# Residual rows turned during the output projection, experts chosen for four groups at once, gate and up weights in 8 KB rows

## What is computed

```python
h = rms_norm(x); q, k, v, u = split(h @ w_in)
x = x + concat(attention(q, k, v, caches), pooling(u)) @ w_o
h = rms_norm(x, ln2_w)
lg = h @ w_rg + b_rg                    # 4 groups
g  = argmax(lg)
le = (h @ w_re + b_re)[group g]         # 4 experts in the group
top_v, top_i = top_k(le, 2)
gates = softmax(lg)[g] * softmax(top_v)
y = x + sum over the two experts e of gates[e] * (silu(h @ w_gate[e]) * (h @ w_up[e])) @ w_down[e]
```

## Time and profile before

| | us |
|---|---|
| median of 3 runs | 1116.34 |
| lowest and highest | 1115.23, 1116.45 |
| the profiled execution | 1114.88 |
| its span in the trace | 1113.0 |
| mean granted TensorE clock | 0.953 |

### The profile page before, as it was taken

How to read it: one execution, slowest core, us unless ns; L and a number is a source line. 1 busy time by engine, 2 the same in 40 slices (tenths; PEclk the granted TensorE clock), 3 DMA queues, 4 the chain that set the end, 5 groups by cost and what they waited for, 6 DMA issues and landing times.

```text
span 1113.0 us, 11421 instructions
## 1 busy us (share of the span) xinstructions
PE 983.6 (88%) x4851; PEld 581.4 (52%) x4851; DVE 268.5 (24%) x396; ACT 142.4 (13%) x325; POOL 19.5 (2%) x38
## 2 busy tenths in 40 slices
PE   5999999999989999999869788876898788978785
PEld 4777888878756667777543223322333233323232
DVE  2007999460423310101260001100010001100011
ACT  3011111211134420110200100000010000001000
POOL 0000000000010000000000000000000000000000
PEclk9999999999989999999969989989898889989898
DMA  9835999865469985284447999999999999999991
GB/s 348 292 127 194 329 404 363 322 252 157 162 243 357 353 312 179 85 302 151 159 195 284 399 389 410 395 408 390 398 400 384 412 387 408 391 399 407 387 372 40
DMA packets 126661, 343.47 MB, mean 309 GB/s; under 512 B 5181, under 2 KB 8439, under 8 KB 116391
## 3 DMA queue, kind: packets, MB, share of 16 engines
q1 hardware_dynamic: 108895, 296.19, 70.6%
q10 hardware_dynamic: 15408, 34.02, 8.3%
q0 software_dynamic: 2304, 12.48, 2.8%
HBM read 330.52 MB, written 11.98 MB: 308 GB/s over the span
## 4 chain that ended last, share of the span: by engine, by line
PE 69%; DMA 21%; SPq 4%; DVE 3%; issue 1%; ACT 1%; POOL 0%; ACTq 0%; DVEq 0%; POOLq 0%
PE PS L739 66%; DMA ring<-in_w_up 13%; SPq L430 4%; DMA ring<-in_w_gate 4%; DMA ring<-in_w_down 4%; PE PS L769 1%; DMA small<-in_small 1%; PE PS L805 1%; PE PS L996 1%; PE PS L754 0%; DVE HT L1479 0%; DVE Z L1479 0%; ACT zT L568 0%; DVE HT L1189 0%; ACT Z L602 0%
## 5 line engine op out<-in xcount | busy, mean ns | idle before, releaser
L739 PE MATMUL PS<-HT,ring 128*128 128x288 f32 x1536 | 382.1, 407 | 1.2 <-issue 0.6
L739 PEld LDWEIGHTS PS<-HT,ring 128*128 128x128 f32 x1536 | 288.3, 190 | 82.8 <-issue 4.9
L739 PE MATMUL PS<-ring,Z 128*64 128x512 f32 (+2 forms) x1072 | 252.7, 614 | 49.7 <-DMA ring<-in_w_up 22.9
L739 PEld LDWEIGHTS PS<-ring,Z 128*64 128x64 f32 (+2 forms) x1072 | 91.3, 146 | 201.3 <-issue 200.4
L739 PE MATMUL PS<-ring,HT 128*64 128x512 f32 x512 | 126.8, 655 | 24.0 <-DMA ring<-in_w_up 10.1
L739 PEld LDWEIGHTS PS<-ring,HT 128*64 128x64 f32 x512 | 44.8, 150 | 102.0 <-issue 102.0
L568 ACT ACTIVATE zT<-PS 128x288 f32<-128x288 f32 x48 | 19.7, 411 | 364.1 <-PE PS L739 364.1
L739 PE MATMUL PS<-Z,X 128*128 128x256 f32 x160 | 46.4, 423 | 9.3 <-DVE Z L1479 3.8
L1479 DVE TENSOR_TENSOR HT<-PS,small 128x512 f32<-128x512 f32 x24 | 16.6, 691 | 142.6 <-PE PS L739 142.6
L1538 DVE TENSOR_TENSOR Z<-Z,PS 128x512 f32<-128x512 f32 x8 | 5.5, 688 | 179.4 <-PE PS L739 179.4
L739 PEld LDWEIGHTS PS<-Z,X 128*128 128x128 f32 x160 | 29.8, 203 | 33.1 <-issue 16.2
(11 more groups left out here) (200 smaller groups left out, 517.9 us busy)
## 6 DMA issues: line engine op xcount, KB each, us to landing
ring<-in_w_gate SPq DMA_DIRECT2D x32, 2048.0 KB, 19.4
ring<-in_w_up SPq DMA_DIRECT2D x32, 2048.0 KB, 19.6
ring<-in_w_down SPq DMA_DIRECT2D x32, 2048.0 KB, 18.9
ring<-in_w_in ACTq DMA_DIRECT2D x12, 2048.0 KB, 17.4
ring<-in_w_o SPq DMA_DIRECT2D x8, 2048.0 KB, 11.7
ring<-in_cache_v SPq DMA_DIRECT2D x8, 1536.0 KB, 7.6
ring<-in_cache_v SPq DMA_DIRECT2D x32, 384.0 KB, 8.6
ring<-in_cache_k SPq DMA_DIRECT2D x24, 384.0 KB, 7.0
```

The lines of the kernel that those rows point to most:

```text
L739: return pe.matmul(out, lhsT, rhs, start=start, stop=stop, skip_group_check=True)
```

## The change

Five things are changed.

1. The residual rows are loaded into columns 2048 to 4095 of `z` (where v and u were) and turned by PE on their own (`turn_rows`), all within the column blocks (`XT_AT` says at which). DVE scales a turned block (`residual_turned`) and adds the projection's column block straight from `zTs` (`column_added`), so the router's product for block n follows three loop steps later and needs no turn of the sum. ACT's copy of block n waits for the sum of block n - 2. SP loads the rows before the second pair of w_o slots, no longer behind it. The square root's table is loaded ahead of the projection, the squares follow each chunk, the root follows the last square; the stores of the last part of x1 and of y's first value come behind the root and behind the logits' copy.
2. The router picks the maximum of the group logits and of each group's four experts in the same five operations, with 60 elements a partition where 12 stood. The second expert of each group is picked while PE makes the index table. The read indices are cast first, straight from PSUM; POOL gathers with them without a copy. The write indices have their own semaphore.
3. The first expert step begins after five of the eight selects; the other three and the gates' table follow its first and second `up`. PE's loop over two turns is written out.
4. Gate and up rows are loaded as four consecutive rows a partition, 8 KB in a row. So `select` takes every fourth column of the gathered rows, and a copy of ln2 in that order (`ln2R`) is loaded by 16 small DMAs at the head of POOL's program.
5. Three memsets of the router are done before the projection.

```diff
-    FIRST_BANKS = (7, 0, 1, 2)
+    FIRST_BANKS = (7, 2, 5, 1)
+    XT_AT = {2: (0, 1), **{n: (n - 1,) for n in range(3, 13)}, 13: (12, 13), 14: (14, 15)}
...
                 for e in range(2):
-                    sp.dma_start(ring[:, s + e, :].rearrange("p (c n) -> p c n", n=TILE),
-                                 w[e].rearrange("a (c p) n -> p (a c) n", p=P)[:, half * 8:half * 8 + 8, :]
+                    sp.dma_start(ring[:, s + e, :].rearrange("p (q n) -> p q n", n=RUN * TILE),
+                                 w[e].rearrange("a (q p c) n -> p (a q) (c n)", p=P, c=RUN)[:, half * 2:half * 2 + 2, :]
...
+        for r in range(4):
+            for q in range(DC // RUN):
+                pool.dma_start(ln2R[32 * r:32 * r + 32, RUN * q:RUN * q + RUN].unsqueeze(2),
...
         pool.wait_ge(x1_stored, 16 * 8)
+        pool.sem_inc(idx_copied, 2)
         for n in range(2):
-            stage_rows(n, 0, n, n + 1)
-            gather(n)
+            gather(n, n)
...
+                if n >= 2:
+                    act.wait_ge(x1T_done, n - 1)
                 block_out(n // 8, n % 8, wo_done, 4)
             if n % 4 == 2 and n > 4:
                 t = n // 4 - 1
-                act.wait_ge(wo_moved, 3 * t + 6)
                 for k, (t0, m) in enumerate(CHUNKS):
+                    act.wait_ge(wo_moved, 3 * t + 4 + k)
...
+                if n == 18:
+                    act.wait_ge(root_in, 8)
+                    act.activation(stat[:, 4:7], stat[:, 4:7], ACT.Sqrt).then_inc(roots, 1)
...
-        for n in range(DC + 6):
+        for n in range(DC + 3):
             if n < DC:
                 column_block(n // 8, n % 8, wo_done, wo_moved, BASE_WO, 4)
-            if 5 <= n < DC + 5:
-                x1_block(n - 5)
-            if n >= 6:
-                router_block(n - 6)
+            for c in XT_AT.get(n, ()):
+                turn_rows(c)
+            if n >= 3:
+                router_block(n - 3)
...
-                ins = mm(PS[:, bank, 256 * i:256 * i + 256], XG[n][:, c * P:(c + 1) * P], SR, True, True)
+                q0 = c // RUN * RUN * P
+                ins = mm(PS[:, bank, 256 * i:256 * i + 256], XG[n][:, q0 + c % RUN:q0 + RUN * P:RUN], SR, True, True)
...
+                if starts:
+                    for j in range(5):
+                        first_select(j)
+                    pe.wait_ge(htg_moved, 4)
...
                 up(k, 0, 4, 0, 1, g0_used)
+                if starts:
+                    for j in range(5, 8):
+                        first_select(j)
+                    pe.wait_ge(htg_moved, 8)
...
                 up(k, 0, 0, 1, 1, gate_done)
+                if starts:
+                    first_gates()
...
+        def column_added(c):
+
+            dve.wait_ge(zT_moved, 2 + 32 + c + 1)
+            dve.wait_ge(xT_moved, c + 1)
+            dve.scalar_tensor_tensor(x1T[:, c, :], zTs[:, c % 2, :], ln2T[:, c:c + 1], x1T[:, c, :],
+                                     ALU.mult, ALU.add).then_inc(x1T_done, 1)
...
+        step(dve.tensor_reduce(m5, L5, AX.X, ALU.max))
+        first_of(one5, L5, m5, best5, 5)
```

More of the change, by code:

```diff
@@ L54 @@
 CAP = 64
+RUN = 4
 NQ = 24
@@ L491, in stage_rows, with gather @@
             pool.wait_ge(idx_copied, nth)
-        def gather(n):
+        def gather(n, at=None):
+            at = 53 + 2 * n if at is None else at
             pool.indirect_dma_start(
                 out=XG[n], out_offset=None, in_=x1_scr,
-                in_offset=bass.IndirectOffsetOnAxis(ap=pidx[:, 53 + 2 * n:54 + 2 * n], axis=0),
+                in_offset=bass.IndirectOffsetOnAxis(ap=pidx[:, at:at + 1], axis=0),
             ).then_inc(gathered[n], 16)
@@ L1055, in turn_gates, with first_select, first_gates, experts @@
             ins.then_inc(sgt_done, 1)
-        def experts(it):
+        def first_select(j):
+            if j >= 4:
+                pe.wait_ge(htg_moved, j - 3)
+            select(0, j, FIRST_BANKS[j % 4])
+        def first_gates():
+            pe.wait_ge(gates_ready, 1)
+            pass_table(0, 4, 128, 232, 16)
+            pe.wait_ge(gates_ready, 2)
+            turn_gates()
+        def experts(it, first=False):
             def up(k, bank, s, w_half, nth, done):
@@ L1121, in experts @@
                 n, second = k // 2, k % 2
-                if not second:
+                starts = first and k == 0
+                if starts:
+                    for j in range(5):
+                        first_select(j)
+                    pe.wait_ge(htg_moved, 4)
+                elif not second:
                     pe.wait_ge(htg_moved, it * 16 + (8 * n + 8))
                 up(k, 0, 4, 0, 1, g0_used)
+                if starts:
+                    for j in range(5, 8):
+                        first_select(j)
+                    pe.wait_ge(htg_moved, 8)
                 if second:
@@ L1152, in _ @@
         pe.wait_ge(sr_ready, 1)
-        for j in range(8):
-            if j >= 4:
-                pe.wait_ge(htg_moved, j - 3)
-            select(0, j, FIRST_BANKS[j % 4])
-        pe.wait_ge(gates_ready, 1)
-        pass_table(0, 4, 128, 232, 16)
-        pe.wait_ge(gates_ready, 2)
-        pe.wait_ge(htg_moved, 5)
-        turn_gates()
-        with pe.Fori(0, 2) as it:
-            experts(it)
+        experts(0, first=True)
+        experts(1)
         pe.wait_ge(idx_ready, 1)
@@ L1348, in _ @@
         dve.tensor_scalar(stat[:, 4:7], stat[:, 0:3], 1.0 / D, EPS, ALU.mult, ALU.add).then_inc(root_in, 1)
-        step(dve.memset(R, 0.0))
         dve.wait_ge(roots, 6)
```

179 lines of the change are left out of this document (96 added, 83 removed).

## The result

| | before | after |
|---|---|---|
| median of 4 runs (us) | 1115.78 | 1091.22 |
| lowest and highest | 1113.64, 1116.45 | 1089.82, 1091.73 |
| profiled execution, its span | 1114.88, 1113.0 | 1091.73, 1089.9 |

After takes 0.9781 of the time of before [0.9764, 0.9798]: 24.6 us less, where 29.7 were forecast. On the chips of the experiments the kernel before ran between 1107 and 1118 us, with medians of 1111.6 (two chips) and 1115.5, and the intervals of the ratios reach 0.25 to 0.4% to either side (0.13 to 0.2% in the last set); where an experiment needs less than that, its trace is read, with times relative to a point within it.

A forecast was written before the change was run, and what follows sets the result against it. Bound: time to the first `up`'s end, then full DMA transfers, then PE's tail. Stream -26.2, front -4.0, head +0.5 give -29.7: 1085.2 us profiled, plus 1.5, 1086.6 median; own bounds 1080.5 to 1090 (0.62), with rivals up to 1097 over 0.9.

The forecast's parts named there:

- the front gives nothing: Rival: x1's store, y and weights hold the gather to 573 us, SP's first issue at 590.5; 1090.6 us, chance 0.20.
- sign of being wrong: Idle DMA mid-experts, select pairs over 1.13 us, 387 GB/s with 8 KB packets, or first gather landing after 573 us.
- signs of being right: Gate and up alone 420 GB/s or more at 1.01; 620-1040 us at 420; SP's load 585-588; projection's last block 549.
- the main term: Expert stream: gate and up rows in 8 KB move at 422 instead of 387 GB/s, 288.1 instead of 314.3 us, -26.2 us.
- PE as the bound: Rival in odd expert steps: weight loads at twice the time, pairs released late; 1092 to 1097 us, chance 0.12.
- 512 B is enough for line rate: Rival for the weight stream: 2 KB rows are as fast as 8 KB; about 1112.8 us, chance 0.03.
- so the stream stays fed: First expert step: second and third release at about 597 and 607 us, pairs in flight lasting to 598 and 608.
- the gather's issue, "no change": Router: +1.4 logits, +0.2 wider operations, -1.1 earlier indices, -0.6 POOL's copy; gather issued at 561.6 us, no change.
- -4.0: Everything before the expert stream: gather +1.9, five select pairs 7.6 us, first `up` -0.8; SP issues at 586.5 us.
- head and tail: Head: 16 small DMAs on POOL, +0.5 us, bounds 0 and +3. Tail: strided selects taken as nothing, at most 2 us.
- The projection's end: Six turns and three router products ahead of the last block: +5.0 us, projection ends at 548.8 us.
- The logits at +1.4: Behind the projection: DVE has the logits at about 555.6 instead of 554.22 us, bounds -1 and +3.

The follow-up runs named there:

- the last set: On one chip, before 1115.48 us: after 1091.74; gather ahead and gates' table later 1085.81; also with part 1 undone and small DMAs late 1082.67.
- selects first: After with part 3 undone, all eight selects and the gates' table ahead of the first expert product: 1095.64 us, ratio 0.9861 to before.
- the pair of experiments: After with part 4 undone (2 KB rows): 1111.43 us, ratio 0.9991; before with part 4 alone (8 KB rows): 1090.73 us, ratio 0.9806.
- weights behind the store: After, with SP issuing the first pair of up weights only when x1's last store has landed: 1090.3 us, ratio 0.9812 to before.
- the three kernels without that wait: After with first up weights behind x1's store (1090.3 us), with them behind the gathers (1087.6), and with part 1 undone (1086.55).
- weights behind the gather: After, with SP issuing the first pair of up weights only when both gathers have landed: 1087.6 us, ratio 0.9787 to before.

## Why the prediction was right, and where it missed

**The range held, its centre did not.** The forecast's own bounds ended at 1090 us. The 1091.2 us measured lie above them, beside the 1090.6 of the first rival, "the front gives nothing". Half of that rival happened: the gather landed at 575.4 us, past the 573 that were named as a sign of being wrong. The other half did not: SP's first load came 3.4 us earlier behind the block, and the time was missing in stream, head and tail. That the number is the rival's is chance. Another sign of being wrong also came, a select pair of 1.32 us where 1.13 was the limit, and the stream did not feel it. Of the signs of being right, the rates came (421 GB/s at 1.01; 422 in the middle), and SP's first load at 589.06 us missed its 585 to 588.

**Right: the bound and the size of the main term.** The stream was to become 26.2 us shorter, priced by the window of down rows. Where no release comes late it takes 447.8 us (selects first) and 447.9 (before with 8 KB rows) instead of 473.9: 25.9 to 26.1 us less. PE as the bound did not come about: at 86% busy the middle runs at 422 GB/s with a share of 1.01. The rule of the Trainium skill (DMA: Bandwidth & Descriptors, section Specifications) that 512 B is enough for line rate would have 2 KB rows as fast; the pair of experiments does not agree, with 387 against 424 GB/s.

**Wrong, 3.2 us: "so the stream stays fed".** The second release was put at about 597 us, with the first pair's bytes lasting to 598, and the third at 607. The comparison left out the time from issue to data, for which I had 1.5 us elsewhere: with it the two pairs' data come at 598.5 and 608.5, half a microsecond late by my own figures. By after's rows SP's second issue came at 600.03, 11.0 us behind the first at 589.06: three selects (3.17), the wait for DVE's scaling (0.78) and `up` (7.09). The third came at 611.45, 11.4 us behind that: the gates' table with its wait for DVE, and a product that ran at a granted clock of 0.76 (603 to 610 us) right behind that wait. I had taken distances of 10.5 and 10. A pair of 4.2 MB lasts 10 us at 422 GB/s, and each microsecond on top is a gap. The two gaps are 1.3 and 1.6 us by the windows. The second goes when the table moves behind the third product; the first stays then (201 GB/s from 594 to 596 us), and neither is there when the selects stay in front.

**Wrong in a part, 0.6 us in the sum: the gather's issue, "no change".** The index chain was counted, the store of x1 was not: the gather needs both. Before, it was issued at 548.39 and its landing was hidden behind the index chain; in after it took 9.94 us and ended 3 us behind the indices. The issue came 2.9 us later behind the block than before (528.7 and 525.8), where no change was forecast. POOL's copy, priced at -0.6, gave nothing either: where the store is out of the way POOL still starts 0.9 us behind the indices (560.57 to 561.51 with the weights behind the store), as it did with the copy (560.68 to 561.66). From the logits' turn to the gather's issue the router's change is worth 0.7 to 0.8 us (7.9 before; 7.1 to 7.2 in the three kernels without that wait), not 1.5. So the first select came 4.5 us later relative to the block (537.6 against 533.1), where +1.9 was forecast. The selects paid for it: 6.5 us from the first select to `up` instead of 12.7 (I had 7.6), and 7.1 instead of 8.8 from there to SP's issue. What they gained beyond my 7.6 and 8.0 us goes with the granted clock. Windows of before's first `up`, of after's five pairs and first `up`, and of the five pairs in the kernel with the weights behind the gather:

```profile
581.72:590.53 8.81, 8.81 (x35) 3.48 (x36) 0.25 (x2) 1.67 (x2) 0.18 (x1) 0.81 0.01 3
```

```profile
575.44:581.93 6.49, 6.49 (x20) 5.53 (x20) 2.77 (x4) 0.00 (x0) 0.00 (x0) 0.72 0.06 27
581.93:589.06 7.13, 7.13 (x34) 2.33 (x33) 0.69 (x1) 0.00 (x0) 0.00 (x0) 1.00 0.00 0
```

```profile
570.78:578.42 7.64, 7.64 (x21) 6.12 (x21) 2.77 (x4) 0.00 (x0) 0.00 (x0) 0.59 0.63 232
```

At a clock of 0.72 the five pairs took 6.5 us, at 0.59 the 7.6 that I had. The front's -3.4 agrees with -4.0 by luck: +2.6 us at the gather and -2.0 at the selects and `up` cancel. The row that showed the danger was read: the earlier trace rows, y's 8 KB packets at 2.12 MB beside 0.81 MB for the 2 KB weights. It was applied to the gather and not to the store that the gather waits for.

**Wrong, 1.4 us each: head and tail.** The head was put at +0.5 within 0 to 3: the small packets cost the loads beside them 37 GB/s over 10 us (380 and 343) and as much before that. I had written 2048 packets; by the pages' counts of those under 512 B (5181 before, 5694 after) there are 513 more. They carry 8 KB. The tail was put at 0 within 0 to 2: 1.1 us of its 1.4 is the stride; the other 0.3 us is not explained.

**The projection's end.** Forecast +5.0, measured +4.9 (544.67 - 35.91; 551.50 - 37.84 is 513.7 against 508.8). The logits at +1.4 came at +0.9 by PE's turn of them. Both terms held; what they were worth to the end was decided elsewhere.

The misses add up: 3.2 + 0.6 + 1.4 + 1.4 = 6.6 us, the difference between -29.7 and -23.1 of the spans. The step that failed most is the release order of the first step, 3.2 of the 6.6.

## What to carry to other kernels

Where windows of one trace show full DMA engines at two rates, the shape of the transfers is the price, and the window with the better shape forecasts what the other would cost, here to within about 1% of the gain. When a faster stream or a reordered start is costed, list for each transfer that a wait needs, also stores, what is issued ahead of it and how much of it there is, and compare each release plus the time from issue to data with the time at which the bytes in flight end. A step moved behind the first product of a loop should be put behind as many releases as its consumer allows.

## What the runs showed of the hardware

- Transfers of 2 KB rows run at 387 GB/s and of 8 KB rows at 421 to 424, both with full DMA engines; 49,152 fewer packets for the same 296.19 MB on SP's queue (108895 and 59743) go with a stream that is 26 us shorter.
- Weight loads with columns 16 bytes apart take 325 ns instead of 196; the earlier trace rows showed no sign of such a price on the moving side, though with no contiguous product of that size beside it.
- The granted clock is at its low level (0.50) when the first selects begin, and in the traces it rises 2.9 to 6.2 us behind the first of them. The same five strided pairs take 6.6 to 7.7 us by that.
- x1's last store takes 9.9 us to land beside 8 KB weight rows, 7.4 beside 2 KB rows (`x_scr<-Z` in after and in after with 2 KB rows), and 2.8 when the weights wait for it.
- Sixteen DMAs of 4-byte elements (512 more packets, 8 KB) lower the rate of the loads beside them from about 380 to 343 GB/s, while the DMA share stays at 1.05.
- PE's first 48 turns take either 6.5 to 7.0 us or 8.8 to 9.1, from one execution of a kernel to the next. Nothing in the traces says why.
